# Four tile slots in a recurrence and a re-shared one-hot build, in a streaming encoder layer on one Trainium2 core

## The reference

```python
att = jnp.where(mask, jnp.einsum('bthk,bshk->bhts', q_in, k_in), 0.0)
o = jnp.einsum('bhts,bshv->bthv', att, vc) + jnp.einsum('bthk,bhkv->bthv', q_in, S)
S = jnp.exp(b_last)[..., None] * S + jnp.einsum('bshk,bshv->bhkv', k_out, vc)
...
o = rms_norm(o, g_gla_out).reshape(B, T, GLA_DV) * jax.nn.silu(zr.astype(jnp.float32))
```

## Time and profile before

| what | value |
|---|---|
| median of 3 runs | 5659.56 us (5651.17 to 5659.95) |
| the profiled execution | 5657.49 us, of which the span of instructions is 5655.9 us |
| stages ahead of the recurrence | 0 to 1912 us |
| recurrence | 1912 to 2224.6 us |
| gated projection, merge, query and first lists | 2224.6 to 3023 us |
| route | 3023 to 3282 us |
| experts and output | 3282 to 5655.9 us |

### The profile page before, as it was taken

One profiled execution on the slowest core, in us unless ns is written; L12 is line 12 of the kernel. 1 busy time (PEld: TensorE's weight loads), 2 busy tenths in 40 slices (PEclk: granted clock), 3 DMA queues, 4 the chain that ended last, 5 costly groups with the idle time before them and its releaser, 6 DMA issues. The chain is left out here.

```text
span 5655.9 us, 61793 instructions
## 1 busy us (share of the span) xinstructions
PE 5059.8 (89%) x23397; PEld 4126.6 (73%) x23397; DVE 3417.3 (60%) x4486; ACT 1746.2 (31%) x2220; POOL 1371.1 (24%) x1059
## 2 busy tenths in 40 slices
PE   8979999999997877989794679999999999978884
PEld 3347888888885544878684669989989999866773
DVE  7742211215664233322558867888888878878887
ACT  7743212122222111121423723333323333223332
POOL 0300000000010122000003723334433334444453
PEclk9989999999998889989897789999999999989997
DMA  9842332233332454433511589999999999999997
GB/s 362 307 150 95 104 100 93 85 108 107 104 104 105 158 192 157 158 99 107 159 45 30 119 326 363 376 377 379 382 376 380 383 378 380 387 378 404 406 406 309
DMA packets 460056, 1334.66 MB, mean 236 GB/s; under 512 B 135869, under 2 KB 193085, under 8 KB 377199
## 3 DMA queue, kind: packets, MB, share of 16 engines
q1 hardware_dynamic: 336180, 667.06, 33.4%
q0 software_dynamic: 96576, 623.69, 28.2%
q10 hardware_dynamic: 27072, 40.91, 2.1%
HBM read 1206.06 MB, written 126.56 MB: 236 GB/s over the span
## 5 line engine op out<-in xcount | busy, mean ns | idle before, releaser
L229 PE MATMUL ps<-w_hi,act_hi 128*128 128x512 f32 x3040 | 1198.7, 394 | 48.7 <-DVE act_lo L1036 23.0
L231 PE MATMUL ps<-w_hi,act_lo 128*128 128x512 f32 x3040 | 1189.2, 391 | 0.0
L230 PE MATMUL ps<-w_lo,act_hi 128*128 128x512 f32 x3040 | 1189.2, 391 | 0.0
L224 DVE TENSOR_TENSOR w_lo<-w_stage,w_hi 128x2048 fp32r<-128x2048 f32 x152 | 348.2, 2292 | 1152.1 <-ACT w_hi L220 1149.7
L2408 ACT ACTIVATE x_hi<-x_stage 128x1024 fp32r<-128x1024 f32 x512 | 543.5, 1061 | 1499.1 <-DMA x_stage<-u_turned 731.2
L2488 DVE TENSOR_TENSOR x_lo<-x_stage,x_hi 128x1024 fp32r<-128x1024 f32 x512 | 625.2, 1221 | 366.9 <-ACT x_hi L2408 363.3
L2335 POOL DMA_INDIRECT u_ring<-u_exp,idx_all x256 | 600.7, 2346 | 872.3 <-DVE u_ring L2506 823.4
L2362 PE MATMUL ps<-act_hi,x_hi 128*128 128x384 f32 x2048 | 694.4, 339 | 58.8 <-DVE x_lo L2488 55.6
L229 PEld LDWEIGHTS ps<-w_hi,act_hi 128*128 128x128 f32 x3040 | 575.1, 189 | 172.5 <-issue 44.0
L2362 PE MATMUL ps<-x_hi,cx_hi 128*128 128x512 f32 x1536 | 613.1, 399 | 96.7 <-DVE cx_lo L2499 79.7
L2363 PE MATMUL ps<-act_lo,x_hi 128*128 128x384 f32 x2048 | 691.3, 338 | 0.0
(11 more groups left out here) (306 smaller groups left out, 5682.4 us busy)
## 6 DMA issues: line engine op xcount, KB each, us to landing
x_stage<-u_turned SPq DMA_DIRECT2D x256, 512.0 KB
x_stage<-v_exp SPq DMA_DIRECT2D x256, 512.0 KB
w_stage<-w_ada SPq DMA_DIRECT2D x96, 1024.0 KB, 6.2
w_stage<-w_in SPq DMA_DIRECT2D x96, 1024.0 KB, 5.2
d_w<-w_buf SPq DMA_DIRECT2D x6, 4096.0 KB, 20.8
gwr<-d_w SPq DMA_DIRECT2D x128, 192.0 KB
d_gw<-gob ACTq DMA_DIRECT2D x128, 192.0 KB
gwr<-d_gw SPq DMA_DIRECT2D x128, 192.0 KB
```

Of the source, the lines that this page charges most:

```text
L224: dve.tensor_tensor(w_lo[:, q % 2], w_in_st[:, q], w_hi[:, q % 2].bitcast(F32), ALU.subtract).then_inc(w_split, 1)
L229: pe.matmul(out, lhs[0], rhs[0], start=first, stop=False)
L230: pe.matmul(out, lhs[0], rhs[1], start=False, stop=False)
L231: return pe.matmul(out, lhs[1], rhs[0], start=False, stop=last)
```

## The change

In the recurrence the three rings have four slots. `o_sb` is gone: `finish` writes its output over `rt` in place, and `turn_o` reads it there. So `load(T)` waits for `turn_o(T - 4)` (`ot_ready`) in place of `post_done` of T - 3, and `finish` waits no more for an `o_sb` slot. The sample states' loads stand behind the load of the sample tile itself (t = 4 in place of t = 2), and the next stage's weights behind the last tile's loads (T = 19 in place of T = 4).

In the route stage the one-hot tables change to ACT 8, DVE 4, POOL 4 for the first key and DVE 12, POOL 4 for the second. `take` runs over a bank key by key, four tokens at a time: it writes runs of four floats into `w_buf` and reads PSUM at a stride of 128 floats; before, it read PSUM in a row and wrote `w_buf` at a stride of 64 floats.

```diff
-        NS = 3
+        NS = 4
...
-        o_sb = sb(st, "o_sb", [P, 2, DVH])
...
                 if T >= NS:
                     sp.wait_ge(o_ready, T - NS + 1)
                     sp.wait_ge(ds_ready, halves_after(T - NS))
-                    sp.wait_ge(post_done, T - NS + 1)
+                    sp.wait_ge(ot_ready, T - NS + 1)
...
-                if t == 2:
+                if t == TP:
                     if h > 0:
                         sp.wait_ge(s_st, 16 * STREAMS * h)
...
-                if T == TP:
+                if T == len(TILES) - 1:
                     for q in range(QPC):
                         load_quarter(sp, c_o0, q, rows(a["w_gla_o"], 0, q))
...
-                    mm = pe.transpose(ps[:, 7, j * P:(j + 1) * P], o_sb[:, T % 2, j * P:(j + 1) * P], ident)
+                    mm = pe.transpose(ps[:, 7, j * P:(j + 1) * P], rt[:, T % NS, j * P:(j + 1) * P], ident)
...
-                if T >= 2:
-                    dve.wait_ge(ot_ready, T - 1)
-                dve.scalar_tensor_tensor(out=o_sb[:, T % 2], in0=ps[:, 2 + T % 2], scalar=ss[:, T, 3:4],
+                dve.scalar_tensor_tensor(out=rt[:, T % NS], in0=ps[:, 2 + T % 2], scalar=ss[:, T, 3:4],
                                          in1=rt[:, T % NS], op0=ALU.mult, op1=ALU.mult).then_inc(post_done, 1)
...
-    FIRST_BY = 5 * ("act", "dve", "pool") + ("act",)
-    SECOND_BY = tuple("pool" if n in (3, 7, 12) else "dve" for n in range(16))
+    FIRST_BY = 4 * ("act", "dve", "act", "pool")
+    SECOND_BY = 4 * ("dve", "pool", "dve", "dve")
...
-                act.activation(w_buf[:, h, :, n0:n0 + 4].rearrange("p c n -> p n c"),
-                               ps[:, 6 + G % 2].rearrange("p (n c) -> p n c", n=4), ACT.Copy).then_inc(w_taken, 1)
+                act.activation(w_buf[:, h, :, n0:n0 + 4], ps[:, 6 + G % 2].rearrange("p (n c) -> p c n", n=4),
+                               ACT.Copy).then_inc(w_taken, 1)
```

## The result

| what | before | changed |
|---|---|---|
| median of 4 runs each, us | 5659.76 (5651.17 to 5668.73) | 5612.37 (5604.51 to 5617.95) |
| profiled execution, span, us | 5655.9 | 5616.4 |
| recurrence, first transposes to last, us | 286.6 | 263.7 |
| route, first id copy to last index cast, us | 227.4 | 209.1 |

The ratio is 0.992, 95% interval 0.9906 to 0.9935: faster, by 47 us where 49 were forecast. The profiled execution of the changed kernel is the slowest of its four runs, which is why the spans lie only 39.5 us apart. The two stages together are 41.2 us shorter, and the recurrence begins 1.4 us sooner. From the last index cast to the end, where no instruction changed, the profiled execution takes 3.7 us more than before; the runs differ by more than that among themselves.

What follows compares the result with a forecast made beforehand. No single engine was full: PE waited for tile loads in the recurrence, ACT and DVE tied in route. From 5657.5 us profiled, -34 and -14 gave 5609.5, or 5611 us with the 2.1 us to the median; range 5584 to 5641.

Steps and rivals of the forecast that it cites:

- The mechanism of the recurrence: Recurrence: old tile waits of 51.5 us go, new waits arise at sample tiles behind the states; sum -34 us.
- The short waits: Recurrence, tiles just before the sample tile: T = 8 waits 0.5 us, T = 9 lands in time; 3 x 0.5 in all.
- The long ones: Recurrence, sample tiles: new waits behind the states, 7 us in three heads and 4.5 in head 3.
- The clock: Recurrence: PE's clock loss after long waits, about 17.6 us before the change and 8 us after.
- the term of T = 9: Recurrence, head 1: loads issued from E + 10.9 (E is the head's start), landed by E + 16.5, no wait.
- The output over `rt`: Recurrence: same operation and shape, cost 0; SP waits on PE's transposes, a few us later in the tile.
- the next weights last: Recurrence: 11 us of loads leave the queue ahead of T = 6 and 7, priced in head 0's old wait; cost 0.
- Route: Route stage: a tile falls from 68.4 to 63 to 64 us, set by DVE; -14 us over three tiles.
- the first rival: Route: the take stays at 1.06 us, stage 0 to 20 us longer, 8 taken; 5634 us, chance 0.22.
- That all waits go: Recurrence rival: the sample tile's loads do not suffer behind the states, -60 us there; 5586 us, chance 0.10.
- That the wait only moves: Recurrence rival: landings at sample tiles 5 to 6 us later each, only -10 us there; 5636 us, chance 0.12.
- The slow take: Route rival: the strided PSUM read makes the take slow, at 2.1 us a tile takes 103; 5730 us, chance 0.06.

Runs made afterwards that it cites:

- e5: Changed kernel with sample states loaded in two halves, streams 0 to 3 behind t = 3, 4 to 7 behind the sample tile; 5600.78 us, 0.9914 of the kernel before.
- e7: Changed kernel with the next stage's weights back behind tile T = 4; 5624.34 us, 0.9951 of the kernel before.
- e10: Changed kernel with five slots, the next weights' last quarter loaded at the next stage's start; 5585.50 us, 0.988 of the kernel before.
- e4: Kernel before with only the route's new shares, the take staying as it was; ratio 1.0009 to the kernel before.
- e11: Changed kernel with four PSUM banks between spread and take in place of two; 5622.09 us, 0.9943 of the kernel before.
- e3: Kernel before with only the new key-by-key take, the shares staying as before; ratio 0.9979 to the kernel before.
- e12: Changed kernel with five slots, four PSUM banks and DVE's four first-key steps given to ACT; 5580.91 us, 0.9874 of the kernel before.
- e9: Changed kernel with each take as two instructions of two tokens, writing runs of two floats; ran once, 5617.05 us.

## Why the prediction came out right, and where its terms were off

The time was 5612 where 5611 was forecast, and that the two agree so closely is luck: the recurrence gave 23 us for 34, the route 18 for 14, and the other 6 of the 47, of which the earlier start is 1.4, are no more than runs differ by. The mechanisms, told below, were right in the main; the sizes were off by about a third in both stages.

*The mechanism of the recurrence was right.* T = 7, 12 and 17 wait no more, T = 8 waits little, and a new wait stands at each sample tile, put there by the states ahead of the loads: forecast 7, 7, 7 and 4.5, measured 7.7, 7.5, 7.5 and 5.6 (28.4 against 25.5). `e5` and `e7` took away and added 2.1 and 4.2 MB ahead of it, and it moved by 5.5 and 11.2 us. That it would be the next thing late is shown.

*Three terms of it were too small or too large*, which make the 11 us. The short waits: I gave 0.5 us to T = 8 and none to T = 9 or T = 4; they are 0.71 + 1.35, 0.55 + 0.52, 0.95 + 0.95 and 1.58, in sum 6.6 against 1.5. The long ones: 2.9 more. The clock: I put its loss at 17.6 us before and 8 after, 9.6 won; the stage without its waits went from 235.1 to 228.7, 6.4 won. In `e10`, which has few long waits left, the same length is 219.4 us, so the changed kernel still lost at least 9.3 us there and the kernel before at least 15.7, if the rest of that difference too is the clock. In the term of T = 9, "issued over 2.3 us and landed by E + 16.5, in time", the issue was right (2001.95, 10.6 us into the head for 10.9) and the landing was not. PE wants the tile 6.9 us after its first issue, which the 5.65 us of idle queues would have met, but it landed after 8.25; at T = 14 and 19 the landing took 7.3 and 8.1 us, with 6.7 and 7.2 to spare, and at T = 4 it took 7.5 with 6.0. In all four the states are issued right behind. That they slow the tile ahead of them is the likely cause, and no run takes it apart. `e10` shows that earlier issue cures it: with a slot more, the waits at T = 8 and 9 are gone in every head.

*The output over `rt`, and the next weights last.* The operation costs what it did, 0.75 us, and PE's transposes too, as forecast. But the slot is held for 4.5 us longer at T = 5, until `turn_o`, and the short waits at T = 8 and 9 are of 0.5 to 1.4 us. I had counted the later issue and not that it would show; no kernel with four slots and an `o_sb` of its own was run. `e7` gives the weights' move its price: 8.7 us of the 23. I had hidden that in "head 0's old wait" and did not name it as a part; head 0 is in fact no shorter (70.9 us against 71.3), since what the weights gave, the states took.

*Route.* The take at 0.592 is the 0.6 that I took, and the first rival is dead as a cost; as a kernel (`e4`) it came out at +2.7 us in the stage where I gave 0 to 20, most likely 8. The tile is 61 to 62 us, not 63 to 64. I let DVE keep its full wait for the ids, 2.8 us a tile; it is 2.2, and the waits for slots, 2.9 a tile, went to 0.1. I had dropped these without saying so and then rounded up. That DVE and not ACT sets the changed tile is supported, though not shown, by `e11`, where freeing PE from ACT gave nothing, and by `e3`, where ACT's 42 us saved gave 8.4. `e12` shows how near the balance is: 5 us taken from DVE gave nothing either, since ACT at once took its place; no run took work off DVE without giving it to ACT.

*The other rivals.* That all waits go was wrong for this kernel, yet `e10` comes near it (8.3 us left) with one slot more. That the wait only moves holds for half of it: 28 us of the 35 that are left are the moved one. The slow take did not happen.

What stays open: I did not try five slots with the states in two halves, which would bear on the 8.3 us that `e10` still waits; and whether the longer short waits in `e5` come from the first half of the states or from the writes before them was not taken apart.

The fastest kernels seen are `e10` and `e12`, 5585.50 and 5580.91 us, 0.988 and 0.9874 of the kernel before in their group.

## What to carry to other kernels

When a ring gets a slot more, ask first what the freed transfer will queue behind: here the loads stopped waiting for their slot and began to wait for 4.2 MB of states ahead of them in the same list. The place in the list can be worth as much as the slot: the states in two halves gave another 20 us of the stage. So large loads go in pieces between the small ones that are needed sooner. Where two engines are tied by a small ring, price two edits together: a shift of work and a cheaper copy were worth +2.7 and -8.4 us alone and -18.3 together.

## What the runs showed of the hardware that was not expected

ACT reads PSUM at a stride of 128 floats at the price of a row: 0.592 us for 128x512 against 0.58 for the plain copy, which writes in a row. It is the write to SBUF that costs: at a stride of 64 floats 1.057 us, in runs of four floats 0.592, in runs of two (128x256) 0.389 against 0.401 plain. The Trainium skill (Advanced Engine Details and Errata, Memory Cachelines) asks for two hits on a 16-byte line of SBUF, and `e9` with exactly two agrees. What it says of PSUM, that every two consecutive elements should be contiguous for best throughput, does not show in ACT's reads here (0.592 us against 0.58).

In `e5` a wait of 2.05 us left the next transposes at 0.66 us, and one of 2.03 us in the next head had them at 1.11:

```profile
2079.51 1.11 PE L1185 MATMUL ps<-kc,qk 128*128 128x128 f32 x4 [2.03 <-DMA rt<-d_r]
```

Waits of some 2 us are thus on either side of the fall of the clock in one and the same stage. Nor does the length of the wait alone decide further up: `e10`'s wait of 3.51 us still left the transposes at 0.66, where the route's groups behind an idle time of 3.15 us ran slow and those behind 2.77 us did not. In the rows above no wait of 1.62 us and below lost it; what PE did before the wait was not varied here, so what decides in between stays open.
